# Third part of the gates in the PEER gating stage: GpSimd makes its products for whole octets

## The reference, cut to what matters

```
s1, i1 = lax.top_k(s[:, :, 0], 16); s2, i2 = lax.top_k(s[:, :, 1], 16)
cand = s1[..., :, None] + s2[..., None, :]          # 8 heads, 256 candidates each
sc, pos = lax.top_k(cand, 16)                        # expert e = i1 * 128 + i2
gate = softmax(sc)                                   # 128 gates for a token
act = gelu(xt . u_tab[e]);  y = sum_e gate_e * act_e * v_tab[e]
```

## Time and profile before

| engine | busy us | share of the span |
|---|---|---|
| PE matmul | 3309.7 | 90% |
| PEld | 2902.9 | 79% |
| DVE | 2234.7 | 61% |
| ACT | 1613.3 | 44% |
| POOL | 158.7 | 4% |

### The profile page before, as it was taken

How to read it: one execution, slowest core, us unless ns; L and a number is a source line. 1 busy time by engine, 2 the same in 40 slices (tenths; PEclk the granted TensorE clock), 3 DMA queues, 4 the chain that set the end, 5 groups by cost and what they waited for, 6 DMA issues and landing times.

```text
span 3664.9 us, 73988 instructions
## 1 busy us (share of the span) xinstructions
PE 3309.7 (90%) x25484; PEld 2902.9 (79%) x25484; DVE 2234.7 (61%) x4659; ACT 1613.3 (44%) x2830; POOL 158.7 (4%) x92
## 2 busy tenths in 40 slices
PE   8979999859999999985999999789879999759997
PEld 2339999847888999985788899677769999758886
DVE  0455886595555688659655574443246885685554
ACT  0113444475444444447554454221134444564453
POOL 0000000000000000000000056110000000000000
PEclk9989999879999999997999999897779999879998
DMA  8644555305556555530565534000034555215653
GB/s 315 202 159 164 181 180 175 115 0 185 193 195 206 170 181 182 172 120 0 183 215 192 200 120 144 13 3 2 2 109 156 183 172 183 69 42 193 205 193 111
DMA packets 143147, 530.07 MB, mean 145 GB/s; under 512 B 16512, under 2 KB 16656, under 8 KB 140752
## 3 DMA queue, kind: packets, MB, share of 16 engines
q1 hardware_dynamic: 140688, 512.96, 41.7%
q0 software_dynamic: 2368, 15.81, 1.1%
HBM read 522.42 MB, written 6.29 MB: 144 GB/s over the span
## 4 chain that ended last, share of the span: by engine, by line
PE 77%; DVE 11%; issue 7%; POOL 2%; ACT 1%; DVEq 1%; DMA 1%; SPq 0%; ACTq 0%; POOLq 0%
PE pS L1505 11%; PE pS L1506 10%; PE pS L1507 10%; PE pY L1577 10%; PE pY L1581 9%; PE pY L1579 9%; PE pS L1456 4%; PE pY L1636 3%; PE pS L1636 3%; POOL lo L1409 2%; PE pS L1558 2%; DVE buf L1025 2%; PE pG L1636 2%; DVE raw L1013 1%; DVE raw L1018 1%
## 5 line engine op out<-in xcount | busy, mean ns | idle before, releaser
L900 DVE TENSOR_TENSOR lo<-raw,hi 128x1024 fp32r<-128x1024 f32 x824 | 1009.1, 1225 | 795.5 <-ACT hi L494 792.3
L494 ACT CAST hi<-raw 128x1024 fp32r<-128x1024 f32 x872 | 913.6, 1048 | 533.6 <-PE pY L1581 507.4
L1505 PE MATMUL pS<-h_hi,hi 128*128 128x256 f32 x3584 | 1023.2, 286 | 48.1 <-DVE lo L900 22.9
L1506 PE MATMUL pS<-h_lo,hi 128*128 128x256 f32 x3584 | 1019.0, 284 | 0.0
L1507 PE MATMUL pS<-h_hi,lo 128*128 128x256 f32 x3584 | 1018.8, 284 | 0.0
L1505 PEld LDWEIGHTS pS<-h_hi,hi 128*128 128x128 f32 x3584 | 692.9, 193 | 55.7 <-issue 52.4
L1506 PEld LDWEIGHTS pS<-h_lo,hi 128*128 128x128 f32 x3584 | 693.1, 193 | 0.0
L1507 PEld LDWEIGHTS pS<-h_hi,lo 128*128 128x128 f32 x3584 | 692.8, 193 | 0.0
L1577 PE MATMUL pY<-hi,h_hi 128*128 128x512 f32 x1536 | 475.1, 391 | 7.9 <-DVE h_lo L1041 7.9
L1581 PE MATMUL pY<-hi,h_lo 128*128 128x512 f32 x1536 | 474.9, 391 | 0.0
L1579 PE MATMUL pY<-lo,h_hi 128*128 128x512 f32 x1536 | 474.7, 390 | 0.0
(11 more groups left out here) (283 smaller groups left out, 3305.6 us busy)
## 6 DMA issues: line engine op xcount, KB each, us to landing
raw<-in_blocks SPq DMA_DIRECT2D x872, 512.0 KB, 3.3
raw<-in_mod_wT SPq DMA_DIRECT2D x48, 512.0 KB, 4.5
buf<-in_mod_wT SPq DMA_DIRECT2D x48, 512.0 KB, 4.4
buf<-in_keysT POOLq DMA_DIRECT2D x3, 1024.0 KB, 5.0
buf<-in_counts SPq DMA_DIRECT2D x1, 2048.0 KB, 14.2
spill_x_res<-buf POOLq DMA_DIRECT2D x2, 1024.0 KB, 5.1
spill_x_h<-buf POOLq DMA_DIRECT2D x2, 1024.0 KB, 7.3
buf<-spill_x_h POOLq DMA_DIRECT2D x2, 1024.0 KB, 7.4
```

Of the source, the lines that this page charges most:

```text
L494: s.copy(hi[slot][:, :, :], raw[slot][:, :, :]).then_inc(hi_ready, 1)
L900: v.tensor_tensor(lo[slot][:, :, :], raw[slot][:, :, :], hi[slot][:, :, :].bitcast(F32), ALU.subtract).then_inc(lo_ready, 1)
L1505: t_.matmul(out, hi[slot][:, c, :], h_hi[:, c, :], start=(c == 0), stop=False)
L1506: t_.matmul(out, hi[slot][:, c, :], h_lo[:, c, :], start=False, stop=False)
```

## The change

The third gate part is taken out of DVE's loop and ACT's loop (`range(3)` becomes `range(2)` in both). POOL now waits for `parts_ready` at the start of each gating stage and then, per octet, for `first_ready` (and from the third octet on for `gates_mm` of the octet two before, which frees the `hots` buffer), and makes the product of the first rows with the third gate part for all 8 tokens in one 128x1024 instruction. PE waits for its semaphore `third_ready` as well. The helpers `spread` and `per_token` move to a place where both engines' programs can call them.

```
+        third_ready = sem("third_ready")
...
+        def spread(x, m):
+            return x.rearrange("p t (a b) -> p t a b", b=2)[:, 0:m]
+        def per_token(x, tok, m):
+            return x[:, bass.ds(tok, m), :].unsqueeze(2).to_broadcast([P, m, P // 2, 2])
...
@@ ACT, gate_rows
-                        for q in range(3):
+                        for q in range(2):
                             i = s.activation(hots[o % 2][:, 1 + q, t, :], first_rows[:, o % 2, t, :], ACT.Copy, scale=picks[q][:, bass.ds(tok, 1)])
...
@@ POOL
+            def third_rows(g):
+                def octet(n, o):
+                    tok = 16 * n + 8 * o if n is not None else 8 * o
+                    pool.wait_ge(first_ready, 2 * n + (N_OCT * g + o + 1) if n is not None else N_OCT * g + o + 1)
+                    if n is not None:
+                        pool.wait_ge(gates_mm, 2 * n + (N_OCT * g + o - 1))
+                    g_.tensor_tensor(spread(hots[o % 2][:, 3], OCTET), spread(first_rows[:, o % 2], OCTET),
+                                     per_token(g_pairs[2], tok, OCTET), ALU.mult).then_inc(third_ready, 1)
+
+                pool.wait_ge(parts_ready, g + 1)
+                octet(None, 0)
+                octet(None, 1)
+                with pool.Fori(0, N_OCT // 2 - 1) as n:
+                    for o in range(2):
+                        octet(n, o + 2)
...
             peer(0)
+            third_rows(0)
             pool.wait_ge(block_done, RING + NQ + NE + 100)
...
             pool.wait_ge(spilled, 64)
+            third_rows(1)
             pool.wait_ge(block_done, RING + L0 + NQ + NE + 40)
...
             peer(2)
+            third_rows(2)
             pool.wait_ge(block_done, RING + K2 + NQ + NE + 40)
...
@@ PE, gate_matmuls
                     pe.wait_ge(rows_gated, done)
+                    pe.wait_ge(third_ready, done)
```

More of the change, by code:

```diff
@@ L1000, in peer @@
                 v.memset(mark[:, 4:5], 0.0).then_inc(parts_ready, 1)
[L1002 to L1006, removed]
                 def onehot_rows(n, o):
```

## The result

The changed kernel takes 3767.64 us (median of four runs, 3766.86 to 3768.78), the kernel before, run beside it, 3664.28 us (median of four): a ratio of 1.028, 95% interval 1.0262 to 1.0298. It is slower by 103 us. The forecast was 3759 us.

What follows compares the result with a forecast made beforehand. DVE's pace was taken to bound the gating stages. Period 4.77 us against 3.71 gives +95 us, head +2, tail -3, together +94 on the median of 3665.3: 3759 us, range 3690 to 3820.

Steps and rivals of the forecast that it cites:

- What bounds the stage: Gating stages: they run at DVE's pace, PE waiting for L1025; period 3.54 us, 3.71 over a whole stage.
- What POOL does to DVE: Gating loop: POOL's whole instruction excludes DVE instructions with two SBUF operands, stalling the first L1018 by 1.63 us an octet.
- POOL's duration: POOL's new 128x1024 bf16 product in each octet: 1.90 us undisturbed, about 2.3 us as recorded.
- The ends of 1.27 and 2.41 us: Low and high durations for POOL's product, giving 3701 us and 3808 us.
- The sum: Three gating stages: period 4.77 us, +95 us over 3 x 30 periods, head +2, tail -3, together +94 us.
- Stall: First L1018 of each octet in the gating stages: DVE held up 1.63 us by POOL's product.
- The head: Start of each gating stage, before the first L1025: 7.28 us against 6.58, +0.7, three times +2 us.
- The tail: End of each gating stage: last matmuls no longer wait for ACT's nine products, about -1.1, three times -3 us.
- (B): Gating loop: POOL gets in only at L1025's start; period 3.64 us at full clock, 3696 us in all; chance 0.13.
- (C): Gating loop: no exclusion for bf16 instructions; DVE runs at 3.14 us an octet, 3623 us in all; chance 0.13.
- (D): POOL's product: 16-bit operands cost double, 3.8 us each; period 6.67 us, 3941 us in all; chance 0.05.
- The clock's effect on the V blocks: Start of the V blocks: a possibly lower clock priced at nothing; 10 us at half speed would cost up to 5 us a stage.

Runs made afterwards that it cites:

- The cost alone: Changed kernel, but DVE still makes its third product too, for 5 tokens, into unused PSUM: 3839.80 us, ratio 1.0476.
- the saving alone: Changed kernel without POOL's product and PE's wait for it; PE takes the second part twice, the third is missing from the result: 3608.09 us, ratio 0.9846.
- the late release: Changed kernel, but POOL waits for onehot (DVE's last product of the octet) instead of first_ready: 3711.73 us, ratio 1.013.
- the two runs with the gates behind the first comparison: Changed kernel with DVE applying octet k-2's gates right after the i1 comparison; 8 tokens on POOL 3703.43 us, 5 tokens 3645.40 us.
- 8 tokens, reordered: Changed kernel, all instructions kept, DVE applying octet k-2's gates after the second comparison, before the products: 3664.02 us, ratio 1.0.
- 5 tokens, reordered: Changed kernel with DVE applying octet k-2's gates after the second comparison, 5 tokens on POOL and 3 on ACT: 3610.89 us, ratio 0.9857.

## Why the prediction was right

**What bounds the stage.** DVE's pace, as read from the earlier trace rows. The cost alone moved the time by 176 us, which follows DVE's sum; the saving alone moved it by 56, of which DVE's sum is 39. One reading on the way was wrong. The list of waits names L1025 for PE, but PE waits for the gates of the octet two before, which were applied one period earlier. What ends its wait is ACT: in the earlier trace rows ACT's nine products end at 753.01 and PE starts at 753.25, and the 29 starts from 723 to 827 us all come 0.23 to 0.28 us after ACT's last product and 1.3 us after DVE's. So the chain from the first comparison through ACT and PE to L1025 is what comes late at the lower clock; at the full clock DVE is busy 10.00 of 10 us and sets the pace, as the prediction says.

**What POOL does to DVE.** The step rested on a few float32 rows of another stage: whole instructions exclude each other when DVE has both operands in SBUF, and a waiting POOL gets in between two DVE instructions. It carried over to bf16 unchanged. The stalled instruction is the first L1019, as named; L1026 stays at 1.21; operands in PSUM make the stall vanish. The condition is too narrow, though. The same stretch of the trace before has DVE instructions with a single tensor as input, in SBUF, that were shut out too:

```profile
2143.82 2.47 DVE L779 TENSOR_SCALAR buf<-buf,mods 128x256 f32<-128x256 f32 x1
...
2148.93 0.40 DVE L779 TENSOR_SCALAR buf<-buf,mods 128x256 f32<-128x256 f32 x1
...
2206.40 2.30 DVE L1171 COPY gT<-buf 128x32 f32<-128x32 f32 x1
...
L1139 DVE SCALAR_TENSOR_TENSOR buf<-pY,buf x160: 360/482/485, 2113.0 to 2253.4; 128x254 f32 x80, 128x255 f32 x80
```

The first three of the eight L779 of the earlier trace rows took 2.33, 2.47 and 2.47 us, one POOL instruction each, the other five 0.40, and a copy of 32 elements took 2.30 us beside a POOL product of 2.40. The 160 L1139, which have one input in PSUM and one in SBUF, never took more than 485 ns (the third number behind their count), although 87 of them lie wholly inside a POOL instruction. So what parts the stretched from the others in these rows is an input in PSUM, not the number of inputs in SBUF. That holds for these forms only; which property of an instruction with one input shuts it out was not tried. It changes nothing in this sum, since the loop has no instruction with one tensor as input. The Trainium skill ("SBUF — State Buffer", "Who interferes with whom") states that a DVE instruction with two SBUF inputs contends with a GpSimd instruction that reads SBUF. This case's traces agree, with 0.48 us grown to 2.18 on two SBUF inputs and 1.22 us unchanged with one in PSUM. Whether a POOL instruction that only writes would leave DVE alone, as that section also says, was not tried.

**POOL's duration.** Taken as 1.90 us from the multiplication with a broadcast operand; undisturbed it is 1.90 us in the late release and with the operands in PSUM. In the changed kernel it is recorded with 2.09 us, not the 2.3 foretold, because it starts 0.95 us after the start of L1014 and not 0.8: the start was taken from ACT's. That cost nothing here, as POOL waits for L1015 either way; a start taken too early is also what spoiled the expectations of the two runs with the gates behind the first comparison. The ends of 1.27 and 2.41 us were both wide of it. The estimate by the Trainium skill's 2.6 cycles an element ("GPSIMD Engine Reference", "Elementwise — side-by-side cycle accounting") would have been 2.2 us; the shorter instructions here (1.26 us for 640 elements) give 1.66 ns an element, 2.0 cycles at the page's 1.2 GHz, and some 0.2 us fixed.

**The sum.** Stall 1.70 us instead of 1.63, period 4.84 instead of 4.77, because I let DVE resume 0.15 us before POOL's end and POOL hide 0.20 us under its wait, each from one row; the octet after the change gives 0.13 and 0.15. Over 90 periods that is 6 us. The head is 7.42 us against 7.28 expected, +0.4 us in all. The tail came out as worked in stage one (865.12 - 862.13 = 2.99 us against 4.15), but the prediction took the other two to be the same, and they were not: before the change their last matmuls ran at the full clock (1.51 us) and the tail was 2.92 us; after it they run at the lower one (2.74 us) and it is 2.99, so the earlier start gains nothing there and the term is -1, not -3. So the stages came to +102.8 us against +94, which is the 9 us by which the forecast was low, two thirds of it the stall. That the medians miss by the same 9 us is luck: stage one began 2.4 us earlier, and the forecast's base (the median of three runs, 1.3 us below the profiled one) and the changed kernel's median (0.8 above its profiled one) make up for it.

**The rivals.** (B), POOL let in only beside the gates, is refuted by the stalled L1019, but its mechanism is what the reordered kernels build on purpose; its price of 3696 us at 1.90 us compares with 3712 for the late release. (C), no exclusion, was 3623 us; the saving alone came to 3608, since (C) had kept the whole of DVE's waits for PE at the lower clock. (D) fell with the duration. The clock's effect on the V blocks was rightly left at nothing: from the end of each stage to the start of the next, and to the end of the span, the two kernels agree within 0.4 us.

## What to carry to other kernels

An idle GpSimd is not free capacity beside a busy VectorE: before work moves there, list which VectorE instructions run at that time and which of them have an operand in PSUM (those with all operands in SBUF, even a single one, were shut out in these traces), and price the move as GpSimd's whole duration less what can lie beside instructions with an operand in PSUM. If such an instruction is in the loop, size GpSimd's piece to it and choose its release so that it asks just before: the same work then cost 160 us, 56 us (8 tokens, reordered) or 3 us (5 tokens, reordered). Look at the trace for one instruction of an ordinary form with an extraordinary duration; a single such row, with its neighbours of usual length, priced this change to within 9 us.

## What the runs showed that I had not expected

- VectorE's order was worth 22 us by itself (3643.04 us without POOL): the period at the granted clock of 0.50 fell from some 3.9 to 3.54 us because VectorE now comes to the application of an octet's gates 7.7 us after the comparison that releases ScalarE, and no longer 5.95.
- GpSimd starts 0.27 us after the end of the instruction that releases it, ScalarE 0.13 to 0.15 us. With a piece of work cut to fit a gap of 1.13 us, that was the difference between 3645 and 3611 us.
- A VectorE comparison of 1024 elements with a float32 operand in PSUM takes 1.21 us against 0.68 with bf16 operands in SBUF, so putting an operand into PSUM to avoid the exclusion returned nothing here (3776.76 us).
